# Delta rule inverse on one Trainium2 core: transposes in TensorE's transposing mode, and 64x64 products on all four quarters of the array

## The reference, cut to what matters

```python
def gated_delta_rule(q, k, v, beta, g):
    ...
    lmat = jnp.where(strict, jnp.einsum('bhnid,bhnjd->bhnij', k_beta, k) * decay, 0.0)
    eye = jnp.eye(CHUNK, dtype=jnp.float32)
    t_inv = lax.linalg.triangular_solve(eye + lmat, jnp.broadcast_to(eye, lmat.shape),
                                        left_side=True, lower=True, unit_diagonal=True)
    u = t_inv @ v_beta
    w = t_inv @ (k_beta * jnp.exp(g_cum)[..., None])
    ...
```

## Time and profile before

| | |
|---|---|
| median of three runs | 2217.13 us (2217.11 to 2217.31) |
| the profiled execution's own time | 2217.3 us |
| its span in the profile | 2215.5 us |
| TensorE matmul busy | 2191.6 us, 99% |
| weight loads busy | 1901.2 us, 86% |
| VectorE busy | 1633.8 us, 74% |
| ScalarE busy | 1309.6 us, 59% |
| mean of DMA traffic | 175 GB/s |

### The profile page before, as it was taken

One profiled execution on the slowest core, in us unless ns is written; L12 is line 12 of the kernel. 1 busy time (PEld: TensorE's weight loads), 2 busy tenths in 40 slices (PEclk: granted clock), 3 DMA queues, 4 the chain that ended last, 5 costly groups with the idle time before them and its releaser, 6 DMA issues.

```text
span 2215.5 us, 35078 instructions
## 1 busy us (share of the span) xinstructions
PE 2191.6 (99%) x13756; PEld 1901.2 (86%) x13756; DVE 1633.8 (74%) x2962; ACT 1309.6 (59%) x2489; POOL 9.2 (0%) x21
## 2 busy tenths in 40 slices
PE   8999999999999999999999999999999999999998
PEld 8888888888888888888888888888888888888886
DVE  7787655677677788755778867777677767699875
ACT  6766345776566666544666655555555655566654
POOL 0000000000000000000000000000000000000000
PEclk9999999999999999999999999999999999999999
DMA  7533333475545555555555555555554555544453
GB/s 267 175 130 115 105 116 123 155 255 198 171 163 190 190 190 190 188 185 191 189 189 190 190 190 189 183 181 183 193 177 163 177 192 188 189 147 139 142 198 124
DMA packets 106613, 388.31 MB, mean 175 GB/s; under 512 B 12064, under 2 KB 12192, under 8 KB 105808
## 3 DMA queue, kind: packets, MB, share of 16 engines
q1 hardware_dynamic: 104688, 377.64, 49.6%
q0 software_dynamic: 1760, 8.42, 1.1%
HBM read 383.30 MB, written 2.13 MB: 174 GB/s over the span
## 4 chain that ended last, share of the span: by engine, by line
PE 93%; DVE 5%; ACT 1%; issue 0%; DMA 0%; DVEq 0%; SPq 0%; ACTq 0%
PE main L487 85%; PE ps L487 7%; DVE WL L881 1%; PE ps L490 1%; DVE PPw L881 1%; ACT PPw L1508 0%; DVE AQ L881 0%; DVE gt L881 0%; ACT WH L1508 0%; DVE XT L881 0%; DVE SM L1353 0%; DVE GQ L887 0%; ACT PP L1508 0%; DVE ROT L881 0%; DVE PTw L1407 0%
## 5 line engine op out<-in xcount | busy, mean ns | idle before, releaser
L1508 ACT ACTIVATE WH<-RAW 128x512 fp32r<-128x512 f32 x1416 | 883.9, 629 | 688.5 <-PE main L487 680.0
L881 DVE TENSOR_TENSOR WL<-RAW,WH 128x512 fp32r<-128x512 f32 x1416 | 961.6, 688 | 372.6 <-ACT WH L1508 363.5
L487 PE MATMUL main<-A,WH 128*128 128x512 f32 (+1 forms) x3680 | 1148.4, 395 | 8.3 <-DVE WL L881 8.3
L487 PEld LDWEIGHTS main<-A,WL 128*128 128x128 f32 x3584 | 675.6, 189 | 154.0
L487 PE MATMUL main<-A,WL 128*128 128x256 f32 x3584 | 715.9, 279 | 0.0
L487 PEld LDWEIGHTS main<-A,WH 128*128 128x128 f32 x3680 | 565.2, 190 | 23.0 <-issue 10.8
L487 PE MATMUL main<-B,WH 128*128 128x512 f32 (+1 forms) x896 | 265.2, 380 | 0.0
L487 PE MATMUL main<-H,WH 128*128 128x512 f32 x704 | 221.3, 396 | 0.0
L487 PEld LDWEIGHTS main<-B,WL 128*128 128x128 f32 x832 | 156.7, 188 | 33.9
L487 PE MATMUL main<-B,WL 128*128 128x256 f32 x832 | 169.3, 279 | 0.0
L487 PEld LDWEIGHTS main<-H,WL 128*128 128x128 f32 x704 | 132.4, 188 | 31.1
(11 more groups left out here) (284 smaller groups left out, 1590.2 us busy)
## 6 DMA issues: line engine op xcount, KB each, us to landing
RAW<-ws SPq DMA_DIRECT2D x708, 512.0 KB, 3.3
CB<-cscr POOLq DMA_DIRECT2D x4, 1024.0 KB, 5.6
xs<-xT SPq DMA_DIRECT2D x8, 256.0 KB, 7.7
XT<-xT POOLq DMA_DIRECT2D x4, 512.0 KB, 8.1
MS<-memT POOLq DMA_DIRECT2D x4, 512.0 KB, 7.6
out<-XT SPq DMA_DIRECT2D x4, 512.0 KB, 2.8
CST<-cst SPq DMA_DIRECT2D x1, 1248.0 KB, 7.6
ROT<-AQ SPq DMA_DIRECT2D x32, 16.0 KB
```

The source lines that it names most:

```text
L487: return e.matmul(o, l, r, start=start, stop=True, skip_group_check=True)
L881: return e.tensor_tensor(o, a, b, op)
L1508: return e.activation(o, i, f, bias=bias, scale=scale, accum_out=accum)
```

## The change

Three things change inside the five levels, and all three engines' lists with them.

- The transpose of `t4` is made by four instructions of TensorE's transposing form (`tr`) on 128x128 pieces, in place of 16 products with the identity. A 128x128 transpose carries a matrix from one partition half into the other. It is now made in all five levels (before, from the second on), into columns 256 to 511 of both banks. The block `cells` is left for the one transpose ahead of the levels.
- The 16 products of `t2^T t4` (`first`) and of `t3^T t0` (`second`) are spread over all four quarters: in each group of four, two stay on the diagonal and two read one partition half and write the other. `first` puts the products of one row half into one bank, `second` brings them back. Both banks are one tensor `two` of 2 by 512 now.
- VectorE and ScalarE read both banks in one instruction each. VectorE makes the next `t2` ahead of the copy of `t3`, and that copy now waits for ScalarE's copy of `t0`, since both read the same banks. In level 1 VectorE has a copy of `t3` more.

```diff
-        Q_PE, Q_VE, Q_AC, Q_MU = 25, 28, 11, 8
+        Q_PE, Q_VE, Q_AC, Q_MU = 21, 29, 11, 8
...
+                def first(l, r):
+
+                    for m in range(4):
+                        for c, s in quarters:
+                            mm(two[rows[s], c, 64 * m:64 * m + 64], l[rows[c], 2 * m + s, :], r[rows[c], 2 * m + s, :])
+
+                def second(l, r):
+
+                    for m in range(4):
+                        for c, s in quarters:
+                            z = mm(two[rows[c], s, 64 * m:64 * m + 64], l[rows[s], 2 * m + c, :], r[rows[s], 4 * c + m, :])
                     z.then_inc(qd_pe, 1)
...
                 for lev in range(1, 6):
                     w.wait_ge(qd_mu, mu + 3 + lev)
-                    w.wait_ge(qd_ve, ve + (17 if lev == 1 else 14 + 2 * lev))
-                    cells(Z, t2, t4)
-                    if lev > 1:
-                        cells(X, t4, K["eye"])
+                    w.wait_ge(qd_ve, ve + 15 + 2 * lev)
+                    first(t2, t4)
+                    for m in range(4):
+                        z = tr(two[:, m // 2, 256 + 128 * (m % 2):384 + 128 * (m % 2)], fl(t4[:, 2 * m:2 * m + 2, :]))
+                    z.then_inc(qd_pe, 1)
                     yield from ticks(2)
                     w.wait_ge(qd_ac, ac + 4 + lev)
-                    if lev > 1:
-                        w.wait_ge(qd_ve, ve + 15 + 2 * lev)
-                    cells(Z, t3, t0)
+                    w.wait_ge(qd_ve, ve + 16 + 2 * lev)
+                    second(t3, t0)
                     yield from ticks(3)
...
                 for lev in range(1, 6):
                     yield from ticks(3)
-                    if lev > 1:
-                        w.wait_ge(qd_pe, pe + 6 + 3 * lev)
-                        e.tensor_copy(t3, eight(X[:])).then_inc(qd_ve, 1)
+                    w.wait_ge(qd_pe, pe + 7 + 2 * lev)
                     if lev < 5:
-                        w.wait_ge(qd_pe, pe + (9 if lev == 1 else 5 + 3 * lev))
                         tt(t2, t1, bm(K[f"lm{lev + 1}"], 8), ALU.mult).then_inc(qd_mu, 1)
+
+                    w.wait_ge(qd_ac, ac + 4 + lev)
+                    e.tensor_copy(halfs(fl(t3)), two[:, :, 256:512]).then_inc(qd_ve, 1)
                     yield from ticks(2)
-                    w.wait_ge(qd_pe, pe + (10 if lev == 1 else 7 + 3 * lev))
-                    tt(t4, t4, eight(Z[:]), ALU.subtract).then_inc(qd_ve, 1)
+                    w.wait_ge(qd_pe, pe + 8 + 2 * lev)
+                    by_half = t4.rearrange("p (m s) j -> p s m j", s=2)
+                    tt(by_half, by_half, two[:, :, 0:256].rearrange("p s (m j) -> p s m j", m=4), ALU.subtract).then_inc(qd_ve, 1)
...
-                    w.wait_ge(qd_pe, pe + (9 if lev == 1 else 5 + 3 * lev))
-                    copy(t0, eight(Z[:])).then_inc(qd_ac, 1)
+                    w.wait_ge(qd_pe, pe + 7 + 2 * lev)
+                    copy(halfs(fl(t0)), twos[0][:, :, 0:256]).then_inc(qd_ac, 1)
```

More of the change, by code:

```diff
@@ L303, in program @@
         slots = [ctx.enter_context(nc.psum_tensor(f"main{i}", [128, 2, 512], F)) for i in range(2)]
-        banks = [None] * 4 + [ctx.enter_context(nc.psum_tensor(f"ps{i}", [128, 512], F)) for i in range(4, 8)]
+        twos = [ctx.enter_context(nc.psum_tensor(f"two{i}", [128, 2, 512], F)) for i in range(2)]
+        banks = [None] * 4 + [twos[i // 2][:, i % 2, :] for i in range(4)]
         off0 = (nc.sbuf_base + 31) // 32 * 32
@@ L608, in octet, with cells @@
             def octet(g):
-                X, Z = banks[4], banks[5]
+                X, Z, two = banks[4], banks[5], twos[0]
                 H, rows = range(4 * g, 4 * g + 4), (slice(0, 64), slice(64, 128))
                 ve, ac, mu = Q_VE * g, Q_AC * g, Q_MU * g
-                def cells(o, l, r):
+                quarters = ((0, 0), (1, 1), (0, 1), (1, 0))
+                def cells(o, l):
                     for n in range(8):
                         for P in rows:
-                            z = mm(o[P, 64 * n:64 * n + 64], l[P, n, :], r[P, n, :] if len(r.shape) == 3 else r[P, :])
+                            z = mm(o[P, 64 * n:64 * n + 64], l[P, n, :], K["eye"][P, :])
+                    z.then_inc(qd_pe, 1)
[7 more added lines that the diff above has]
+                            z = mm(two[rows[c], s, 64 * m:64 * m + 64], l[rows[s], 2 * m + c, :], r[rows[s], 4 * c + m, :])
                     z.then_inc(qd_pe, 1)
@@ L656, in octet @@
                 w.wait_ge(qd_ve, ve + 14)
-                cells(X, t3, K["eye"])
+                cells(X, t3)
                 yield from ticks(3)
@@ L660, in octet @@
                     w.wait_ge(qd_mu, mu + 3 + lev)
-                    w.wait_ge(qd_ve, ve + (17 if lev == 1 else 14 + 2 * lev))
-                    cells(Z, t2, t4)
-                    if lev > 1:
-                        cells(X, t4, K["eye"])
+                    w.wait_ge(qd_ve, ve + 15 + 2 * lev)
+                    first(t2, t4)
+                    for m in range(4):
+                        z = tr(two[:, m // 2, 256 + 128 * (m % 2):384 + 128 * (m % 2)], fl(t4[:, 2 * m:2 * m + 2, :]))
+                    z.then_inc(qd_pe, 1)
                     yield from ticks(2)
                     w.wait_ge(qd_ac, ac + 4 + lev)
-                    if lev > 1:
-                        w.wait_ge(qd_ve, ve + 15 + 2 * lev)
-                    cells(Z, t3, t0)
+                    w.wait_ge(qd_ve, ve + 16 + 2 * lev)
+                    second(t3, t0)
                     yield from ticks(3)
-                w.wait_ge(qd_ve, ve + 26)
+                w.wait_ge(qd_ve, ve + 27)
                 for b, o in enumerate((X, Z)):
@@ L677, in octet @@
                 yield from ticks(2)
-                w.wait_ge(qd_ve, ve + 28)
+                w.wait_ge(qd_ve, ve + 29)
                 for n in range(8):
@@ L1161, in octet @@
                     yield from ticks(3)
-                    if lev > 1:
-                        w.wait_ge(qd_pe, pe + 6 + 3 * lev)
-                        e.tensor_copy(t3, eight(X[:])).then_inc(qd_ve, 1)
+                    w.wait_ge(qd_pe, pe + 7 + 2 * lev)
                     if lev < 5:
-                        w.wait_ge(qd_pe, pe + (9 if lev == 1 else 5 + 3 * lev))
                         tt(t2, t1, bm(K[f"lm{lev + 1}"], 8), ALU.mult).then_inc(qd_mu, 1)
+                    w.wait_ge(qd_ac, ac + 4 + lev)
+                    e.tensor_copy(halfs(fl(t3)), two[:, :, 256:512]).then_inc(qd_ve, 1)
                     yield from ticks(2)
-                    w.wait_ge(qd_pe, pe + (10 if lev == 1 else 7 + 3 * lev))
-                    tt(t4, t4, eight(Z[:]), ALU.subtract).then_inc(qd_ve, 1)
+                    w.wait_ge(qd_pe, pe + 8 + 2 * lev)
+                    by_half = t4.rearrange("p (m s) j -> p s m j", s=2)
+                    tt(by_half, by_half, two[:, :, 0:256].rearrange("p s (m j) -> p s m j", m=4), ALU.subtract).then_inc(qd_ve, 1)
                 yield from ticks(3)
                 for b, o in enumerate((X, Z)):
-                    w.wait_ge(qd_pe, pe + 23 + b)
+                    w.wait_ge(qd_pe, pe + 19 + b)
                     e.tensor_copy(GV[:, h4, 128 * b:128 * b + 128], four(o[:])).then_inc(qd_ve, 1)
@@ L1636, in octet @@
                     yield from ticks(5)
-                    w.wait_ge(qd_pe, pe + (9 if lev == 1 else 5 + 3 * lev))
-                    copy(t0, eight(Z[:])).then_inc(qd_ac, 1)
+                    w.wait_ge(qd_pe, pe + 7 + 2 * lev)
+                    copy(halfs(fl(t0)), twos[0][:, :, 0:256]).then_inc(qd_ac, 1)
                 yield from ticks(7)
-                w.wait_ge(qd_pe, pe + 25)
+                w.wait_ge(qd_pe, pe + 21)
                 for c, o in enumerate((X, Z)):
```

## The result

The changed kernel takes 2204.57 us (median of 4 runs, 2204.46 to 2204.85) against 2217.15 for the kernel before: 12.6 us less, a ratio of 0.9943 with a 95% interval of 0.9931 to 0.9955. The forecast was 2205.1. The profiled execution took 2204.85 us, with a span of 2203.0, 12.5 under the one before.

The account below looks back on a forecast made before the run. TensorE, busy 99% of the span, was taken to bound the kernel. From 2217.3 us, 12.4 saved over two octets and 0.4 of waiting added gave 2205.3, or 2205.1 as a median; the range was 2203.1 to 2210.8.

Parts of the forecast that it names:

- The bound: Whole kernel: TensorE busy 99% of the span, so time taken off it is time off the kernel unless it then waits.
- The levels' sum: Five levels of each octet: 2.05 us per level, 10.2 per octet where it was 16.42; two octets save 12.4 us.
- Four quarters: Blocks `first` and `second`: 32 matmuls on four quarters take 0.465 us, half of the 0.93 on two.
- Handed out too slowly: TensorE's instruction queue in a block: 14.5 ns per load and matmul needed, fastest sustained pace 29; judged not the limit.
- The transposes: Each level, behind `first`: four 128x128 transposes cost 0.435 us, 0.109 each.
- The change of shape: TensorE around each block: going from the full array to quarters and back costs 0.34 us.
- The chain through VectorE: `second` waiting for VectorE's copy of `t3`: margin 0.1 us in level 3; 0.4 us of waiting over the first octet.
- Four quarters no faster: Rival for the blocks: something shared holds 32 matmuls at 0.93 us; time 2214.0; chance 0.11.
- Partly faster: Rival for the blocks: half the gain, 0.70 us per block, by handing out or first weight loads; about 2209.8; chance 0.12.
- Slower by the engines taking turns: Rival for the levels: late `t3` copies make TensorE stand 1.97 us in each of ten; time 2224.8; chance 0.03.
- The range: Kernel time from 2203.1 (no waiting, cheaper shape changes) to 2210.8, said to include 3.5 us of waiting and "Partly faster".
- the second rival: The rival "Partly faster": a block takes 0.70 us, 20 blocks give back 4.7 us; about 2209.8; chance 0.12.

Follow-up runs that it names:

- ident4: The changed kernel with each level's four 128x128 transposes made as 16 identity products on all four quarters, right behind `first`: 2205.70 us.
- runs4: The changed kernel with all four products of a quarter in a row before the next quarter gets any: 2221.34 us.
- no_tr: The changed kernel without its four transposes per level, so the transpose of `t4` is missing: 2201.71 us.
- split: The kernel before with its 16 identity products one half of the weight stream later in levels 2 to 5, so they stand alone: 2219.95 us.
- copy_first: The changed kernel with VectorE's copy of `t3` put back ahead of the product for the next `t2`: 2204.84 us.
- paired orders: The changed kernel with block products ordered two quarters at a time, paired by diagonal, row half or column half: 2210.05, 2210.18 and 2210.55 us.
- p_row: The changed kernel with block products ordered by pairs of quarters sharing a row half, one pair after the other: 2210.18 us.
- p_col: The changed kernel with block products ordered by pairs of quarters sharing a column half, one pair after the other: 2210.55 us.
- runs2: The changed kernel with two products in a row on each quarter before the next quarter gets any: 2205.88 us.

## Why the prediction was right, point by point

- **The bound.** TensorE's time was the kernel's time. From the initial block of the first octet to the last block of the second the kernel before ran from 137.00 to 311.04 us and the changed one from 137.17 to 298.64: 174.04 against 161.47, 12.57 less. That is the whole gain; nothing after it gave any back.
- **The levels' sum.** 2.05 us per level was forecast, 1.20 + 0.82 = 2.02 is measured (rounds of 1.90 and 1.52, less 0.70 each). It is this close in part because two errors cancel: a block is a little dearer than its term, the transposes a little cheaper. One of the signs was wrong: a block was to take 0.5 to 0.6 us from its start to the transposes, and takes 0.63 (162.36 to 162.99), since the way back lies in between.
- **Four quarters.** This was the term of which the trace before showed nothing. A block was taken at 0.465 us; `second` costs 0.82 with its stay, which is 0.48 beside the forecast 0.34. Group 8 of the rows carried the inference rightly: row halves free of one another and column halves free of one another meant four free quarters. The rounds of ident4 bear it out. What the prediction did not see is that this holds in the order written, which alternates the quarters with each product. Its working never used the order: for the order of runs4 it would have given the same 2205.1 us, and that took 2221.3. That the kernel had the good order was luck, as far as the prediction goes. "Handed out too slowly" was weighed as a rate and is not a limit as such; the limit is how much one quarter may have waiting, and runs4 shows that it can cost more than the change gains.
- **The transposes.** Forecast 0.435 us for four; no_tr gives 0.38 to 0.39. The term was 0.05 too large: behind a stay on quarters four of them add less than 4 x 0.109. Why is not shown.
- **The change of shape.** 0.34 us forecast; in split 0.33 by rounds, 0.30 by time and 0.35 by the stretch over both octets.
- **The chain through VectorE.** In level 3 the prediction left 0.1 us to spare, and measured is a wait of 0.1; copy_first removes it and no_tr makes it longer. Allowed for were 0.4 us over the octet. That is 0.3 of the 0.5 us by which the forecast was above the time; about as much again is the 0.02 to 0.03 us by which each of the ten levels was put too high.
- **The rivals.** Four quarters no faster (2214.0): rounds with `second` would have stayed at 1.97. Partly faster (2209.8): the changed kernel isn't there. The paired orders are, at 2210, by handing out as this rival had it, though not as a rate: the order of the list does it. Slower by the engines taking turns: TensorE's only new wait is the 0.1.
- **The range.** Its lower end, 2203.1, is a sum of terms; its upper end, 2210.8, is not. It lies 1.0 above the second rival, and the two things it names, both at full size, would give 2204.7 + 4.7 + 3.5 = 2212.9.

The Trainium skill's rule in "TensorE: Matmul & The Clock Gate", part 3, that a weight load overlaps running matmuls only where the row group differs, is not borne out: p_row, whose pairs share a row half, is as fast as p_col (2210.18 and 2210.55 us), and a block with both quarters of each row half at work takes 0.48 us, where taking turns would keep it at 0.93. The floor of about 25 ns between starts in part 1 of the same page does not hold across quarters either, where 32 starts in a block take under 0.5 us.

## What to carry to other kernels

Where products of 64x64 stand in a TensorE-bound stretch, put them on all four quarters and alternate the quarters with every product: the same 32 matmuls took half the time (0.48 us for 0.93), and with each quarter's products in a row they were slower than on two quarters. To see whether that can pay, look in the trace for two row halves that run beside one another and two column halves that do, and take their paces as the bounds. A product with an identity is no longer dear once it is on four quarters (0.46 us for a block, beside 0.38 to 0.39 for four transposes); choose the transposing form for where it puts the result, here the other partition half, which lets a whole level cross and come back.

## What the runs showed of the hardware that was not expected

- Matmuls are handed out in list order, but each quarter has its own row of waiting ones: one running and three waiting explains the paired orders (+0.29 us per block) and forecast runs4 (+0.86, worked out +0.84). It fits every order tried except for the last 0.02 us in runs2.
- Each quarter keeps its pace whatever the other three do: it starts a matmul every 58 ns with two quarters at work and with four, a block of 32 on four costs 0.48 us, and the mean record of a matmul stays at 222 to 224 ns.
- Going from the full array to quarters and back costs 0.30 to 0.35 us for each stay, 20 stays in the levels of the changed kernel, 6 to 7 us. Sharing those stays between the two octets was not tried.
